# Stick-breaking heads: sums over later key blocks formed on GpSimd ahead of the matmuls

## The reference, cut to what matters

```
def _stick_breaking_attention(q, k, v):
    ...
        strict = kpos[None, :] < qpos[:, None]
        z = jnp.einsum('bhqd,bhkd->bhqk', qb, k).astype(jnp.float32) * scale
        log_fail = jnp.where(strict, jax.nn.log_sigmoid(-z), 0.0)
        after = lax.cumsum(log_fail, axis=3, reverse=True) - log_fail
        weights = jnp.where(strict, jnp.exp(jax.nn.log_sigmoid(z) + after), 0.0)
        return jnp.einsum('bhqk,bhkd->bhqd', weights.astype(v.dtype), v)
```

## Time and profile before

| | |
|---|---|
| median of 3 runs | 1966.43 us (1961.6, 1966.43, 1966.61) |
| the profiled execution | 1966.65 us, of which span 1964.9 us |
| PE busy | 1858.9 us (95%) |
| DVE busy | 1069.4 us (54%) |
| ACT busy | 832.9 us (42%) |
| GpSimd busy | 130.7 us (7%) |
| mean granted clock of TensorE | 0.977 of full speed |

### The profile page before, as it was taken

How to read it: one execution, slowest core, us unless ns; L and a number is a source line. 1 busy time by engine, 2 the same in 40 slices (tenths; PEclk the granted TensorE clock), 3 DMA queues, 4 the chain that set the end, 5 groups by cost and what they waited for, 6 DMA issues and landing times.

```text
span 1964.9 us, 24248 instructions
## 1 busy us (share of the span) xinstructions
PE 1858.9 (95%) x8948; PEld 1432.2 (73%) x8948; DVE 1069.4 (54%) x1640; ACT 832.9 (42%) x1393; POOL 130.7 (7%) x164
## 2 busy tenths in 40 slices
PE   6787999999999879989999999989999999999997
PEld 3686778888888656657888888857766776866675
DVE  6696454444433557756444443465465466555637
ACT  4221344444222457644434432232366633246753
POOL 7533000000000000000000000000000000100000
PEclk9978999999999999999999999999999999999999
DMA  4311223223333211112322233322211121211111
GB/s 166 105 42 41 97 86 97 96 96 96 98 91 101 65 29 29 44 41 86 107 96 96 96 90 98 95 72 86 76 52 49 50 86 65 87 65 54 54 35 62
DMA packets 56828, 151.18 MB, mean 77 GB/s; under 512 B 15745, under 2 KB 20641, under 8 KB 56737
## 3 DMA queue, kind: packets, MB, share of 16 engines
q1 hardware_dynamic: 55232, 148.31, 23.9%
q0 software_dynamic: 1504, 1.64, 0.3%
HBM read 143.83 MB, written 4.19 MB: 75 GB/s over the span
## 4 chain that ended last, share of the span: by engine, by line
PE 84%; DVE 10%; ACT 4%; issue 1%; DMA 0%; POOL 0%; DVEq 0%; SPq 0%; ACTq 0%
PE bank L1836 18%; PE bank L1837 17%; PE bank L1838 17%; PE bank L2320 3%; PE bank L2322 3%; PE bank L2321 3%; PE bank L2297 2%; PE bank L2283 1%; PE bank L2282 1%; PE bank L2281 1%; PE bank L2041 1%; DVE wl L1096 1%; DVE G L1136 1%; PE bank L2069 1%; PE bank L2406 1%
## 5 line engine op out<-in xcount | busy, mean ns | idle before, releaser
L1096 DVE TENSOR_TENSOR wl<-raw,wh 128x1024 fp32r<-128x1024 f32 (+3 forms) x280 | 324.1, 1158 | 533.5 <-ACT wh L583 531.0
L583 ACT ACTIVATE wh<-raw 128x1024 fp32r<-128x1024 f32 (+3 forms) x280 | 279.0, 996 | 597.9 <-PE bank L1838 524.0
L1836 PE MATMUL bank<-xH,wh 128*128 128x512 f32 x896 | 359.5, 401 | 11.3 <-DVE wl L1096 9.4
L1837 PE MATMUL bank<-xL,wh 128*128 128x512 f32 x896 | 351.5, 392 | 0.0
L1838 PE MATMUL bank<-xH,wl 128*128 128x512 f32 x896 | 351.5, 392 | 0.0
L1836 PEld LDWEIGHTS bank<-xH,wh 128*128 128x128 f32 x896 | 170.2, 190 | 53.6 <-issue 15.3
L1837 PEld LDWEIGHTS bank<-xL,wh 128*128 128x128 f32 x896 | 170.1, 190 | 38.9 <-issue 4.1
L1838 PEld LDWEIGHTS bank<-xH,wl 128*128 128x128 f32 x896 | 169.8, 190 | 35.9
L1836 PE MATMUL bank<-hidH,wh 128*128 128x512 f32 x352 | 137.3, 390 | 0.0
L1838 PE MATMUL bank<-hidH,wl 128*128 128x512 f32 x352 | 136.9, 389 | 0.0
L1837 PE MATMUL bank<-hidL,wh 128*128 128x512 f32 x352 | 136.9, 389 | 0.0
(11 more groups left out here) (424 smaller groups left out, 3313.1 us busy)
## 6 DMA issues: line engine op xcount, KB each, us to landing
raw<-w_gu_dram SPq DMA_DIRECT2D x88, 512.0 KB, 3.4
raw<-w_p_dram SPq DMA_DIRECT2D x64, 512.0 KB, 3.4
raw<-w_dn_dram SPq DMA_DIRECT2D x32, 448.0 KB, 3.3
raw<-w_glu_dram SPq DMA_DIRECT2D x16, 512.0 KB, 3.5
raw<-w_dn_dram SPq DMA_DIRECT2D x16, 512.0 KB, 3.5
raw<-w_out_dram SPq DMA_DIRECT2D x16, 512.0 KB, 3.4
raw<-w_in_dram SPq DMA_DIRECT2D x8, 512.0 KB, 7.5
raw<-w_o_dram SPq DMA_DIRECT2D x8, 512.0 KB, 3.5
```

Of the source, the lines that this page charges most:

```text
L583: nc.scalar.activation(wh[:, (st.base + u) % 2, 0:kts * P], raw[:, (st.base + u) % 4, 0:kts * P], ACT.Copy).then_inc(w_high, 1)
L1096: nc.vector.tensor_tensor(wl[:, s, 0:kts * P], raw[:, (st.base + u) % 4, 0:kts * P], wh[:, s, 0:kts * P].bitcast(F32), ALU.subtract).then_ ...
L1836: nc.tensor.matmul(bank, wh[:, s, w], hi[:, k, :], start=first and kt == 0, stop=False)
L1837: nc.tensor.matmul(bank, wh[:, s, w], lo[:, k, :], start=False, stop=False)
```

## The change

GpSimd adds up, in a new tile `later` (128 partitions, 2 sides, 3 x 128 columns), the blocks of later keys that meet the same queries. Columns 0 to 127 hold blocks 2 + 3 for the queries of block 3; columns 128 to 255 hold blocks 1 + 2 for the queries of block 2; columns 256 to 383 hold block 1 plus the first of these sums, for the queries of block 3. PE then needs one matmul with `minus8` for each query column of a key block in place of one for each later key block: with `sp` for the queries of the next block, with `later` for those beyond. Over the key blocks of a head these matmuls cover 384 + 256 + 128 = 768 columns; before it was 768 + 384 + 128 = 1280. The tile lies on the memory of `cq_exact` and half of `ck_exact`, so GpSimd first waits for the last softmax shares; for the second pair it also waits for the sums of the first.

```
+    later_mem = Region(nc, mix.base + mix.at, 4 * KB)
...
+    later = later_mem.tensor("later", [P, 2, 3 * P])
...
+                def add_later(side, to, a, b):
+                    return nc.gpsimd.tensor_tensor(later[:, side, to:to + P], sp[:, side, a:a + P], b, ALU.add)
+
+                pool.wait_ge(sem("shares_ready"), 2 * STEPS * (layer + 1))
+                for p in range(2):
+                    for side in range(2):
+                        pool.wait_ge(sem("stick_soft"), 12 * layer + 6 * p + side + 1)
+                        if p:
+                            pool.wait_ge(sem("stick_sums"), 12 * layer + 6)
+                        add_later(side, 0, SOFF[2] + P, sp[:, side, SOFF[3]:SOFF[3] + P]).then_inc(sem("stick_later"), 1)
+                    for side in range(2):
+                        pool.wait_ge(sem("stick_soft"), 12 * layer + 6 * p + side + 3)
+                        pool.wait_ge(sem("stick_later"), 8 * layer + 4 * p + side + 1)
+                        add_later(side, P, SOFF[1] + P, sp[:, side, SOFF[2]:SOFF[2] + P])
+                        add_later(side, 2 * P, SOFF[1] + 2 * P, later[:, side, 0:P]).then_inc(sem("stick_later"), 1)
...
                             nc.tensor.matmul(o, const("from_here"), sp[:, side, SOFF[k]:SOFF[k] + S - k * P],
                                              start=False, stop=False, skip_group_check=True)
-                            for m in range(k + 1, QT):
-                                nc.tensor.matmul(o[:, (m - k) * P:S - k * P], const("minus8"), sp[:, side, SOFF[m]:SOFF[m] + S - m * P],
+                            if k < 3:
+                                nc.tensor.matmul(o[:, P:2 * P], const("minus8"), sp[:, side, SOFF[k + 1]:SOFF[k + 1] + P],
+                                                 start=False, stop=False, skip_group_check=True)
+                            if k < 2:
+                                pe.wait_ge(sem("stick_later"), 8 * layer + 4 * p + 2 * (1 - k) + side + 1)
+                                terms = slice(0, P) if k else slice(P, 3 * P)
+                                nc.tensor.matmul(o[:, 2 * P:S - k * P], const("minus8"), later[:, side, terms],
                                                  start=False, stop=False, skip_group_check=True)
```

## The result

The changed kernel took 1959.22 us (median of 20 runs, 1953.15 to 1963.18), the kernel before 1966.52 us (20 runs, 1959.96 to 1969.75). The ratio is 0.9965, with a 95% interval from 0.9958 to 0.9973, so the change saves about 6.9 us, 0.35%. The forecast was 1959.7 us. The interval reaches 0.9973, so the timed runs alone don't settle whether the gain is above the 0.3% that the prediction took as the bound.

A forecast was written before the change was run, and what follows sets the result against it. PE was taken as the bound, full over the stick heads. The profiled 1966.65 us minus 6.9 for removed columns, with added work priced at nothing, gave 1959.75, stated as 1959.7 us; range 1956 to 1963.

The forecast's parts named there:

- What bounds the kernel: Over the stick heads PE is busy for all 50.00 of 50 us, so every column not streamed should shorten the program.
- What is removed: Products with the constant matrix: 0.65 us a head for key block 0, 0.21 for key block 1; 6.9 us in all.
- The waits on PE: Sixteen matmuls wait for GpSimd's sums; waits long fulfilled were priced at nothing.
- The sums on GpSimd: 24 sums of 128x128 float32, six for each pair of heads, at 0.78 us each, ready before PE needs them.
- the 8.7 us that were thought to be spare: First pair: time between the last sums' end at 1529.3 us and PE coming to key block 0's product at about 1538.0.
- What the sums do to DVE: GpSimd's sums can hold up DVE's masks and sums with two SBUF operands; priced at nothing, uncovered up to 12.4 us.
- The bound of 3.1 us: Most that four sums could hold DVE up before the masks of unit 1, against a margin of 4.2 us.
- What is late next: ACT's weights before the second product with the values: 1.62 us spare become 0.32; priced 0; rival up to 2.6, chance 0.10.
- The clock: Rival, chance 0.12: after layer 0's norm PE's clock rises sooner or later in the work, giving 1957.3 or 1962.1 us.
- the 2.4 us that were allowed for: Gain, or about as much loss, if PE's clock rise after layer 0's norm falls elsewhere in the work.
- The spread of the runs: Rival, chance 0.07: two new runs are of the kind 4.8 us shorter, giving 1955 us.
- The slower rival: GpSimd's sums late: PE waits from 2.8 us a sum, all gain lost from 3.1; 1970.2 us at 3.27; chance 0.05.

The follow-up runs named there:

- The matmuls alone: Changed kernel without GpSimd's sums and PE's waits for them, the narrower matmuls reading the softplus tile instead: 1958.64 us, ratio 0.997.
- the kernels with more gain: Kernel before without any product with the -8 matrix: 1951.31 us; also with the product with the values one output slice later (1949.79) or a weight split moved back (1947.82).
- The experiment with key block 0 alone: Changed kernel, but only key block 0 uses the sums and key block 1 keeps its 256 + 128 columns: 1960.38 us, ratio 0.9978.
- three kernels that should agree: Changed kernel (1959.22 us); the same without sums and waits (1958.64 us); the same with two GpSimd fills ahead of each sum (1958.62 us).

## Why the prediction was right

- **What bounds the kernel.** PE's columns, in both windows. The matmuls alone gave the whole gain.
- **What is removed.** 0.86 us a head was worked out, 6.9 us in all; 6.77 came, and the single kernels gave 2.57 a layer for key block 0 (2.60 was worked out). That the median of the runs came within 0.5 us of the forecast is finer than a spread of 10 us allows, and in part luck; the 6.77 against 6.9 is the better test.
- **The waits on PE.** Priced at nothing from the output products; the interval with and without them is 104.31 us.
- **The sums on GpSimd.** Taken at 0.78 us each, the upper of the two nearest sizes; most take 0.46, but the bound was too low, as one takes 0.83 and one 1.45. The six sums of the first pair, timeline of GpSimd in the changed kernel, with DVE's rows at the same time behind them:

```profile
1520.32 0.45 POOL L567 TENSOR_TENSOR later<-sp 128x128 f32<-128x128 f32 x1 [142.94 <-DVE sp L1822]
1521.77 0.46 POOL L567 TENSOR_TENSOR later<-sp 128x128 f32<-128x128 f32 x1 [1.00 <-DVE sp L1822]
1524.03 0.46 POOL L567 TENSOR_TENSOR later<-sp 128x128 f32<-128x128 f32 x1 [1.80 <-DVE sp L1822]
1524.44 0.46 POOL L567 TENSOR_TENSOR later<-sp,later 128x128 f32<-128x128 f32 x1
1525.73 0.83 POOL L567 TENSOR_TENSOR later<-sp 128x128 f32<-128x128 f32 x1 [0.82 <-DVE sp L1822]
1526.52 1.45 POOL L567 TENSOR_TENSOR later<-sp,later 128x128 f32<-128x128 f32 x1
...
1524.45 0.87 DVE L1819 TENSOR_TENSOR sp<-sp,sl 128x384 f32<-128x384 f32 x1
...
1525.56 0.68 DVE L1784 TENSOR_TENSOR gL<-T,gH 128x512 fp32r<-128x512 f32 x1
1526.38 1.26 DVE L1114 TENSOR_TENSOR wl<-raw,wh 128x1024 fp32r<-128x1024 f32 x1
```

  The last takes 1.45 us, since it starts beside DVE's weight split of 1.26 us and ends after it. It ends at 1527.97; PE comes for its result at 1537.41, so the 8.7 us that were thought to be spare cover it.
- **What the sums do to DVE.** In this pair one of DVE's sums (L1819) is longer, 0.87 us where it was 0.56; in each of the other pairs one or two are, by 0.2 to 0.3 us. The mask of unit 1, second side, comes 0.3 us later against the last transposes (11.29 us after them where it was 10.98), and PE uses it 3.7 us after that. The bound of 3.1 us was ten times too high for this pair, on the safe side.
- **What is late next.** Right in place and size: 0.32 and 0.31 us to spare, as worked out, and the kernels with more gain ran into it.
- **The clock.** It rose after the norm of layer 0 as before: 4.8 us after the first product in both profiles. So that rival didn't come up in this pair, but it is real: over the thirteen profiles of this study the rise came 3.1 to 5.7 us after that product. It is worth less than the 2.4 us that were allowed for: the unchanged stretch behind it, 225.07 us before, took 224.8 to 225.4. What moves the rise is open.
- **The spread of the runs.** One of the twenty runs, at 1953.15 us, was of the short kind; the median didn't move. The experiment with key block 0 alone was profiled in such a run (1954.37 us, where its median is 1960.38), and its first place lies at 1509.7 us, the earliest of all. So the short time came from ahead of the stick heads, from a cause that no run here isolates.
- **The slower rival.** Its threshold was wrong, though it wasn't needed. It put the first loss at sums of 2.8 us each, waited for by PE; with a sum every 2.4 to 2.6 us (two of the twelve in layer 0 took 3.1 and 3.5) PE already waited, 0.5 us a layer, and for DVE. The path of the trouble is GpSimd's reads, then DVE's softplus, then PE, and it opens before the sums themselves are late: in the first pair the sixth ended at 1538.65, and PE came for it at about 1540. The weak step is the one that worked out GpSimd's lateness alone. It kept DVE's hold-up at one short sum for each meeting, where long sums hold DVE up for their own length, and it looked at DVE's masks of unit 1 only, not at those of unit 2, where the wait came up.

## What to carry over

Where an engine is full and a neighbour idle, adding up on the neighbour what the full one multiplies by the same constant in float32 saves its columns one for one, as long as the sums are ready before they are due, and as long as they are short enough not to make the neighbour's neighbour late (here VectorE, which waits while GpSimd reads). Work out how much room the next chain has before widening such a gain: here 1.6 us became 0.3, and moving the waiting product only moved the wait, while shortening the chain removed it. And when one run differs from the next by more than the change is worth, measure between two instructions on either side of it in the trace.

## What the runs showed of the hardware

- A DVE instruction with two SBUF operands waits for a running GpSimd instruction that reads SBUF (0.56 us became 1.74 beside a sum of 1.68) and not for one that only fills (0.56 us beside fills of 1.75). It works in the other direction too: a GpSimd sum of 0.46 us took 1.45 beside a DVE split of 1.26.
- Three fp32r matmuls of 128 columns in a row took 0.29 us, and two of 256 with one of 128 took 0.30, while a single one of 128 behind a float32 matmul took 0.06. A float32 matmul of 128 columns took 0.22.
- The time spent ahead of an unchanged place, 1509.7 to 1519.2 us from the start of the span, varies more between executions than this change is worth, while the 104 us behind it agree to 0.01 us in three kernels that should agree.
- After 5.7 us without work PE ran at the lower clock, with starts 0.43 us apart, and the rise to the upper one came 3.1 to 5.7 us after the first product, at different points in thirteen profiles of nearly the same program.
